# A hybrid encoder trunk on one core: the first stage's order of units, turns and side work changed

## The reference

```python
xn = rms_norm(x, norm1)
proj = xn @ w_in                    # 1536 hyena columns, then q, k, v
y_hy = hyena_mixer(hy_in, ...)      # width-3 conv, x1*v, long filter by FFT, times x0
y_at = window_gqa(q, k, v, ...)     # 8 heads, |q-k| <= 128
mixed = concatenate([rms_norm(y_hy), rms_norm(y_at)])
h = x + mixed @ w_out
gate, up = split(rms_norm(h, norm2) @ w_gate_up)
return h + (silu(gate) * up) @ w_down
```

## Time and profile before

| | |
|---|---|
| median of 3 runs | 2723.38 us (2722.14 to 2725.51) |
| the profiled execution | 2724.04 us, its span in the trace 2722.3 us |
| busy share | PE 96%, PE weight load 88%, DVE 77%, ACT 50%, POOL 45% |
| chain that ended last | PE 84%, DVE 7%, DMA 4%, issue 2% |
| `front` | from 0 to about 820 us of the span |

### The profile page before, as it was taken

The page is one execution under the profiler, slowest core; times in us unless marked ns, Lnnn a source line. Parts: engine busy times, 40 slices in busy tenths (PEclk is TensorE's granted clock), DMA queues, the critical chain, the costliest instruction groups (busy, mean ns, idle before and its releaser), DMA issues.

```text
span 2722.3 us, 39455 instructions
## 1 busy us (share of the span) xinstructions
PE 2619.3 (96%) x13881; PEld 2394.6 (88%) x13881; DVE 2106.0 (77%) x2518; ACT 1372.8 (50%) x2375; POOL 1230.2 (45%) x1182
## 2 busy tenths in 40 slices
PE   8999999999898999999999999899999989999998
PEld 6888989888797888878999999899999989999997
DVE  6765664678448777867888888988888888888887
ACT  5564544477448787764343434443434443443432
POOL 1655211112112454465687764455554444444443
PEclk9999999999998999999999999999999999999999
DMA  7688967899996454455444443543333355333332
GB/s 232 194 281 233 318 208 222 278 287 277 249 223 181 128 146 126 127 163 156 131 139 140 138 119 121 185 139 113 113 112 102 93 182 159 91 92 89 90 90 89
DMA packets 470044, 446.33 MB, mean 164 GB/s; under 512 B 54670, under 2 KB 377358, under 8 KB 469559
## 3 DMA queue, kind: packets, MB, share of 16 engines
q1 hardware_dynamic: 441960, 372.22, 47.4%
q0 software_dynamic: 27888, 71.58, 8.4%
HBM read 329.90 MB, written 113.79 MB: 163 GB/s over the span
## 4 chain that ended last, share of the span: by engine, by line
PE 84%; DVE 7%; DMA 4%; issue 2%; SPq 2%; ACT 1%; POOL 0%; DVEq 0%; ACTq 0%; POOLq 0%
PE ff_banks L85 17%; PE ff_banks L86 17%; PE ff_banks L87 17%; PE pr_acc L85 4%; PE pr_acc L86 4%; PE pr_acc L87 4%; PE am_mix L85 2%; PE am_mix L87 2%; PE am_mix L86 2%; PE pr_gen L85 2%; PE am_turn L2359 2%; PE pr_gen L87 1%; PE pr_gen L86 1%; DMA sp_k<-k_dram 1%; PE am_score L2346 1%
## 5 line engine op out<-in xcount | busy, mean ns | idle before, releaser
L3494 DVE TENSOR_TENSOR ff_h<-ff_h,ff_banks 128x1536 f32<-128x1536 f32 x231 | 402.9, 1744 | 6.2 <-PE ff_banks L87 5.4
L3330 ACT COPY ff_r<-ff_banks 128x384 f32<-128x384 f32 x198 | 94.9, 479 | 593.2 <-PE ff_banks L87 593.1
L3477 DVE TENSOR_TENSOR ff_dlo<-ff_dlo_raw,ff_dhi 128x512 fp32r<-128x512 f32 x231 | 212.8, 921 | 173.4 <-ACT ff_dhi L3360 173.1
L85 PE MATMUL ff_banks<-ff_xhi,ff_ghi 128*128 128x384 f32 x924 | 313.5, 339 | 13.8 <-DVE ff_silu L3454 8.1
L85 PE MATMUL pr_acc<-pr_xhi,pr_whi 128*128 128x386 f32 (+1 forms) x864 | 305.2, 353 | 12.7 <-DVE pr_xlo L1682 7.7
L87 PE MATMUL ff_banks<-ff_xhi,ff_glo 128*128 128x384 f32 x924 | 311.7, 337 | 0.0
L85 PE MATMUL ff_banks<-ff_xhi,ff_uhi 128*128 128x384 f32 x924 | 310.8, 336 | 0.7 <-ACT ff_r L3330 0.6
L86 PE MATMUL ff_banks<-ff_xlo,ff_ghi 128*128 128x384 f32 x924 | 311.2, 337 | 0.0
L86 PE MATMUL ff_banks<-ff_xlo,ff_uhi 128*128 128x384 f32 x924 | 310.6, 336 | 0.0
L87 PE MATMUL ff_banks<-ff_xhi,ff_ulo 128*128 128x384 f32 x924 | 310.0, 335 | 0.0
L3178 POOL TENSOR_TENSOR ff_act<-ff_act,ff_silu 128x384 f32<-128x384 f32 x99 | 116.6, 1177 | 419.6 <-issue 234.1
(11 more groups left out here) (353 smaller groups left out, 6692.2 us busy)
## 6 DMA issues: line engine op xcount, KB each, us to landing
ff_glo_raw<-w_gate_up SPq DMA_DIRECT2D x132, 256.0 KB, 3.0
ff_ulo_raw<-w_gate_up SPq DMA_DIRECT2D x132, 256.0 KB, 3.0
ff_dlo_raw<-dsum_dram SPq DMA_DIRECT2D x132, 256.0 KB, 2.7
pr_raw<-w_in SPq DMA_DIRECT2D x108, 256.0 KB, 5.8
ff_dlo_raw<-w_down SPq DMA_DIRECT2D x99, 256.0 KB, 2.6
sp_k<-k_dram SPq DMA_DIRECT2D x64, 256.0 KB, 5.6
pr_xs<-x SPq DMA_DIRECT2D x18, 512.0 KB, 5.7
xkeep_dram<-pr_xs SPq DMA_DIRECT2D x18, 512.0 KB, 4.5
```

What stands on the lines that cost most here:

```text
L85: pe.matmul(out, still[0], moving[0], start=start, stop=False, skip_group_check=goes_on)
L3330: act.copy(kept[n][:], bank(X)).then_inc(copied, 1)
L3477: dve.tensor_tensor(dlo[d_slot(n)][:], din[d_slot(n)][:], dhi[d_slot(n)][:].bitcast(F32), ALU.subtract).then_inc(d_low, 1)
L3494: dve.tensor_tensor(to, to, lowered_all(k), ALU.add).then_inc(added, 1)
```

## The change

**Order of the first two units.** The first two units of a round are now worked by chunks: (unit 0, c 0), (unit 1, c 0), (unit 0, c 1), (unit 1, c 1), instead of unit by unit. `turn(r, 3)`, `turn(r, 4)`, `turn(r, 5)` and the peek each stand later against the slots, and `weights` of the third unit stands one event before it is used, where it stood two. The bank of `acc` goes by the event's number instead of by c.

```diff
+    def abreast(r, i):
+
+        return i < 2
+
+    def place_of(r, i, c):
+        return i // 2 * 4 + 2 * c + i % 2 if abreast(r, i) else 2 * i + c
...
+            for at, (i, c) in enumerate(order):
+                n = first_unit(r) + i
+                if n + 1 < UN and c == (abreast(r, i) and i % 2):
+                    weights(n + 1)
+                now[0] = event(r, i, c)
+                u_turn(now[0])
+                first_half(r, i, c)
+                if at == 0:
+                    turn(r, 3 if r else 4)
+                    if goes_on:
+                        norm(GT * r + GT)
+                if at == 1:
+                    turn(r, 5 if r else 6)
+                if c and 1 <= i <= 4 and goes_on:
+                    squares(GT * r + GT + i)
...
+                second_half(r, i, c)
...
+                if c and 1 <= i <= 4 and goes_on:
+                    scale(GT * r + GT + i)
+                evict(r, i, c)
+                if at == 0:
+                    turn(r, 4 if r else 5)
+                if at == 1 and r and peeks(r):
                     turn(r, 6)
```

**The seam's wait.** The wait at a round's start no longer counts the two clears of rounds 2 and 5:

```diff
-    def edge_lows(r, seam=True):
-
-        return sum((0, 1, 3, 2, 1, 3)[k] + 2 for k in range(1, r + 1)) - 2 * (not seam)
+    def edge_lows(r):
+
+        return sum((0, 1, 3, 2, 1, 3)[k] + 2 for k in range(1, r + 1)) - 2 * (not peeks(r))
```

**The peek kept.** In rounds 0 and 1 ScalarE and VectorE write the peeked column's high and low part into a small tile `peeked` too, and rounds 3 and 4 copy it from there instead of from the next tile that came back from DRAM:

```diff
+    peeked = Place(nc, "pr", 227616).sb("peeked", [P, 2, NG - 1, KT], F32R)
...
+                    if rd >= NG:
+                        dve.tensor_copy(xlo[:, ks, o], kept_here.bitcast(F32)).then_inc(x_low, 1)
+                        continue
```

```diff
-        while now[0] < 2:
-            yield
+        yield
         wave(0, 0)
...
+            if t in (0, N2):
+                yield
...
+            sp.wait_ge(weighted, NTT)
+            sp.dma_start(prompt_u[:], u_rows[LS:T].rearrange("(t p) c -> p t c", p=P)).then_inc(skip_in, 16)
...
+                if j == 1:
+                    for t in range(2):
+                        octet_parts(t)
+                        yield
         first_z()
+        yield
+        yield
```

170 lines of the change are left out of this document (91 added, 79 removed).

## The result

The changed kernel takes 2729.63 us (median of 11 runs, 2725.53 to 2732.41) beside 2722.14 us of the kernel before (11 runs, 2716.81 to 2725.51): ratio 1.0023, interval 1.0016 to 1.0031. It is slower, by 6 us going by the ratio (7.5 between the medians), where 33 us of gain were forecast. The profiled execution is 2727.64 us for a span of 2725.8.

What follows compares the result with a forecast made beforehand. TensorE was taken to bound the kernel, with gains only from its waits before 820 us and the slowed clock behind them. Eight terms sum to 33.3 us, so 2724.0 becomes 2690.7, typically 2690 us; range 2678 to 2708.

Steps and rivals of the forecast that it cites:

- the prediction's bookkeeping: Each removed TensorE wait of 2.4 us or longer also saves 1.6 to 2.0 us of slow matmuls.
- Round 4: Turn into round 4: two waits and slow matmuls go, 10.6 us, less a new VectorE wait of 4.4; gain 6.2.
- Round 2: Wait at 290.79 goes with its slow matmuls; unit 1's weights come 0.9 us late; gain 3.2 us.
- Opening: Opening and waves: the wait for tile 5 goes, a 1.4 us wave wait comes, later waits shrink; gain 5.5 us.
- round 1: Turn of round 1: the 2.81 us wait at 160.44 goes with 1.6 of slow matmuls; gain 4.4 us.
- the filter's tile: Filter's 17th tile: a free slot puts one half ahead of the 2.5 us wait for `fi_h`; gain 2.2 us.
- the 2.66 that the prediction cites: Opening, ScalarE: cited cost in us of a table switch with its drain; two extra switches would be 5.3 us.
- Round 3: The 4.21 us peek wait at 391.24 goes with 2.0 of slow matmuls; 0.8 us wait stays; gain 5.4.
- Product steps: Product steps one slot earlier against the eviction give `sp_k` 2 to 3 us more before use; gain 2.0 us.
- the transfers set the pace: Rival, chance 0.15: TensorE's gains from round 3 on are given back since the same bytes move; 18 us less, 2708.
- Round 5: Two more halves stand ahead of the first inverse step: 4.4 us of the `ir_z` wait goes, some 3.8 stay.
- VectorE takes over: Rival, chance 0.07: VectorE bounds the opening and round 4, so their 5.5 and 6.2 us go; 2702 us.
- Slower: Rival, chance 0.05: TensorE waits for a late eviction at each of 14 product steps, costing 62 us; 2752.

Runs made afterwards that it cites:

- peek_sooner: Changed kernel with the peek column's copy ahead of the eviction of unit 1, chunk 0, in rounds 3 and 4: 0.9993 of the kernel before.
- products_later: peek_sooner with product step 0 three slots later and octets 0 and 1 back behind product steps 0 and 1: 0.9973 of the kernel before.
- turn_products_later: products_later with all rounds taken unit by unit: 0.9979 of the kernel before.
- units_in_turn: Changed kernel with all rounds taken unit by unit, all else kept: 0.9986 of the kernel before.
- waves_old_place: products_later with the waves back at their old place, three slots later: 1.0017 of the kernel before.
- before_later2: Kernel before the change with product step 0 and all side work behind it two slots later: 0.9987 of the kernel before.
- later_alone: products_later without its peek edit, so the peek column stands behind the eviction again: 0.9986 of the kernel before.
- tile17_early: products_later with four tile loads of each round, tile 17 among them, issued one turn sooner: 0.9975 of the kernel before.
- octets_back: Changed kernel with the parts of octets 0 and 1 back behind product steps 0 and 1, without their own slots: 1.0007 of the kernel before.

## Why the prediction was wrong

**The way of reading held in part, the places it looked at were too few.** The clock's part can be counted: sum over windows of 5 us of length x (1 - granted clock), 0 to 820 us, is the time that slow matmuls add. With the waits:

| | waits | clock | sum | front, less 824.0 |
|---|---|---|---|---|
| before | 57.3 | 29.0 | 86.3 | 0 |
| the change | 64.3 | 27.4 | 91.7 | +2.3 |
| peek_sooner | 61.7 | 18.8 | 80.5 | -5.2 |
| products_later | 57.9 | 20.5 | 78.4 | -7.9 |
| turn_products_later | 59.7 | 16.2 | 75.9 | -10.6 |

The sums follow the ends of `front` to about 3 us here (all lists reach to 820 us, so the sooner kernels' take in some of the next stage); for units_in_turn and waves_old_place they are 4 and 6 us off. The prediction took the gain to be a shorter list, by 25 us. In the best version the list is as long as before, and what is shorter is the clock's part: the mean granted clock of all executions says so too, 0.9880 against 0.9858, some 6 us of the 7 that the ratio gives. (The kernel before's profiled execution has 0.984, less than its mean of 0.9858, so that its 29.0 is by an estimate from the two some 5 us above the typical.) Waits of over 2.4 us sum to 35.1 us before (11 of them), to 34.6 in the changed kernel (6) and to 17.6 in products_later (5). It is tempting to call that the reason, but it isn't shown: before_later2 has 31.3 us in nine such waits and its clock's part is 17.0. Nor is 2.4 us a limit, as the prediction's bookkeeping had it: in the kernel before the granted clock was under 1 in the 2 us behind waits of 1.26 and 2.20 us (65.87 and 86.32), and stayed at 1.00 behind one of 2.55 (234.22).

Much of what was booked was won and lost again. The prediction added its terms as if each, once won, stays won ("a gain is a wait that goes, less one that comes"). But the versions stand 7.6 us ahead to 1.3 behind the kernel before at half 64, and 2.4 ahead to 3.0 behind at half 80. The best version, products_later, is still 26 us short of the forecast, and turn_products_later, which has neither late eviction, 28.

*Round 4 is the step that failed.* "I book a new wait of 4.4", for VectorE's queue between the first product step and the peek. Measured: 11.93. With the peek ahead of the eviction the wait is 4.19. That this meets the 4.4 is partly luck: VectorE did have its 16 us of work, from 509.25 to 525.3, but 3.3 of them are what its subtractions lose beside GpSimd (3.48 and 3.56 us where 1.28 and 2.49 are usual), which the sum did not have. What the step left out was ScalarE's queue, where the eviction that the new order moves one event ahead needs a buffer whose store stands on SyncE behind twelve loads. I had counted how long each engine's work takes and not what each moved instruction waits for. Moving the peek column, in rounds 3 and 4, took 0.30% back, and moving the product steps with the octets' loads behind the store 0.37% (later_alone); the two overlap.

*Round 2*, booked at -3.2, was +5.8. The step named tile 17's norm, but as work ahead of the weights on VectorE, 0.9 us; it was ScalarE that stood 5.07 us until the tile had landed. And in tile17_early, where that wait is gone, the 3.9 us won were given back by half 80.

*The prompt's table*, 5.24 us, stood in no term: the side work's being sooner was counted as a gain, and not asked when its next transfer would land.

*Opening, round 1, the filter's tile*: right in sign, 5.7 us of 12.1. The wait at 31.67 is gone and the wave's wait is 0.81 where 1.4 was booked. A wait of 2.41 at 78.71 for an eviction and one of 1.99 at 158.76 took part of it. ScalarE did switch its table eight times up to round 1 instead of six, 1.28 us each, and the next operation starts at most 0.02 us behind the load (46.04 and 47.34, 53.76 and 55.05): a switch took 1.3 us here, and the 2.66 that the prediction cites are not seen. *Round 3*: 2.8 of 5.4; the peek's wait is 1.45, booked at 0.8.

*Product steps*, booked at -2.0, were +7.0. Seven waits of 0.5 to 0.6 us for `pr_rt` are new, and the largest piece, in the changed kernel, is this one:

```profile
572.46 0.76 PE L85 MATMUL pr_gen<-sp_ahi,pr_g 128*128 128x512 f32 x1 [4.68 <-DVE sp_pb L1934]
```

Every version lost 3.5 to 11.1 us on the kernel before between halves 144 and 176: products_later went from -15.1 to -9.5, before_later2 from -8.5 to -3.8, turn_products_later from -10.2 to -6.5, and octets_back, which was not ahead, from +1.0 to +8.6. The rival "the transfers set the pace" would bring them to one time at half 176; they stand there from -9.5 to +8.6. VectorE's waits for `sp_k`, 550 to 690 us, are 17.9 us in the changed kernel and 15.9 before, at 267 and 280 GB/s, while 356 GB/s were moved from 290 to 300 us. So the transfers have a part, but that they set the pace is not shown, and the cause of the +7.0 stays open.

*Round 5* and the z rows: 2.2 of 4.4. "What goes is two halves of 2.21" counted on the path through the z rows' transfers, and there are indeed two slots more ahead of them. But 7.31 us stayed where 3.8 were booked, because the path was now another: the eviction of unit 1, chunk 0, that waits 7.65 us for its store. It is round 4's mistake again, and the kernels that take round 5 unit by unit, with the z rows in the same slots, wait 1.20 us.

The rivals: "VectorE takes over" was right about round 4 in part, and its 2702 took everything else as won. "Slower" named an eviction behind every product step; no such wait is in the list, so that its 0.05 did not foresee what came. What made the kernel slower than before was the eviction of unit 1, chunk 0: with round 4's out of the way it is at 0.9993 to 1.0003, and round 5's costs some 6 us in the trace. A chance of 0.05 for slower was too low for a change that moves instructions past each other on four in-order queues.
